# A mixture-of-experts step on one core: buffers in another order, expert homes at multiples of 512 bytes

## What is computed

```python
x = x + gate1 * (mix @ p['w_out'])          # mix: attention | RWKV-7 | HGRN2
h = rms_norm(x, p['norm_ffn_g']) * (1.0 + scale2) + shift2
x = x + gate2 * moe(h)                      # 32 experts, top 4 of them per token
# one expert: gu = xblk @ moe_w_gu[e] + b; act = clamped SwiGLU(gu); act @ moe_w_down[e] + b
```

## The kernel before

| buffer | before | past a multiple of 512 | after | past a multiple of 512 |
|---|---|---|---|---|
| `chosen` (new, 384 bytes) | - | - | 1152 | 128 |
| `ring` (6 homes) | 1152 | 128 | 1536 | 0 |
| `const_sb` | 99456 | 128 | 183808 | 0 |
| home 6 in `const_sb` | 99968 | 128 | 183808 | 0 |
| `param_sb` (2 homes) | 127872 | 384 | 99840 | 0 |
| `proj` (2 homes) | 160640 | 384 | 148992 | 0 |
| `spare` (1 home) | 195456 | 384 | 132608 | 0 |
| `h_nat`, `x_res` | 211840, 220032 | 384 | 212224, 220416 | 256 |

## Time and profile before

### The profile page before, as it was taken

How to read it: one execution, slowest core, us unless ns; L and a number is a source line. 1 busy time by engine, 2 the same in 40 slices (tenths; PEclk the granted TensorE clock), 3 DMA queues, 4 the chain that set the end, 5 groups by cost and what they waited for, 6 DMA issues and landing times.

```text
span 1219.7 us, 17160 instructions
## 1 busy us (share of the span) xinstructions
PE 1151.0 (94%) x7144; PEld 463.6 (38%) x7144; DVE 331.4 (27%) x682; ACT 213.3 (17%) x381; POOL 44.4 (4%) x76
## 2 busy tenths in 40 slices
PE   4999989889999999999999999999999999999996
PEld 0435578755333333333333333333333333333332
DVE  1203777744221111221122111122112211111112
ACT  1212264412111111111111111111111111111112
POOL 0300200000000000000000000000000000000000
PEclk9999999999999999999999999999999999999999
DMA  9999200399999999999999999999999999999994
GB/s 370 324 364 393 79 2 10 147 399 394 406 428 426 426 426 429 426 429 427 427 428 428 427 427 428 428 427 429 426 430 426 429 429 427 426 430 427 427 428 189
DMA packets 44446, 458.91 MB, mean 376 GB/s; under 512 B 5284, under 2 KB 7500, under 8 KB 16624
## 3 DMA queue, kind: packets, MB, share of 16 engines
q1 hardware_dynamic: 41328, 451.46, 88.4%
q0 software_dynamic: 2592, 5.67, 1.6%
q10 hardware_dynamic: 480, 1.13, 0.2%
HBM read 456.76 MB, written 1.47 MB: 376 GB/s over the span
## 4 chain that ended last, share of the span: by engine, by line
PE 74%; DMA 14%; DVE 5%; SPq 4%; issue 2%; ACT 1%; another core or an unknown queue 0%; DVEq 0%; ACTq 0%
PE bank L1308 29%; PE bank L1331 15%; DMA ring<-in_moe_w_gu_dram 12%; PE bank L655 7%; SPq L413 4%; PE bank L1266 4%; PE bank L1250 4%; PE bank L1065 2%; PE bank L1288 2%; DMA ring<-in_w_mod_dram 2%; DVE const_sb L2277 1%; PE bank L630 1%; PE bank L1258 1%; PE bank L643 1%; PE bank L775 1%
## 5 line engine op out<-in xcount | busy, mean ns | idle before, releaser
L1308 PE MATMUL bank<-ring,proj 128*64 128x512 f32 x1024 | 227.8, 594 | 12.7 <-DMA ring<-in_moe_w_gu_dram 12.0
L2268 DVE TENSOR_SCALAR const_sb<-bank 128x512 f32<-128x512 f32 x32 | 22.1, 692 | 426.3 <-PE bank L1308 426.3
L1308 PEld LDWEIGHTS bank<-ring,proj 128*64 128x64 f32 x1024 | 71.8, 137 | 164.8 <-issue 135.1
L1331 PE MATMUL bank<-param_sb,const_sb 128*64 128x512 f32 x512 | 116.9, 598 | 4.8 <-DVE const_sb L2277 4.8
L1331 PE MATMUL bank<-ring,const_sb 128*64 128x512 f32 x512 | 116.9, 598 | 4.8 <-DVE const_sb L2277 4.8
L1694 ACT ACTIVATE const_sb<-const_sb 128x512 f32<-128x512 f32 x32 | 20.2, 630 | 577.0 <-DVE const_sb L2268 577.0
L1308 PE MATMUL bank<-proj 128*64 128x512 f32 x512 | 115.3, 592 | 0.0
L2282 DVE TENSOR_TENSOR x_res<-bank,x_res 128x512 f32<-128x512 f32 x64 | 41.2, 686 | 246.7 <-PE bank L1331 246.7
L655 PE MATMUL bank<-ring,param_sb 128*128 128x512 f32 (+2 forms) x224 | 88.4, 550 | 0.0
L1308 PEld LDWEIGHTS bank<-proj 128*64 128x64 f32 x512 | 36.8, 137 | 73.1 <-issue 73.1
L1266 PE MATMUL bank<-x_res,const_sb 64*128 64x512 f32 x256 | 63.6, 615 | 0.9 <-DVE x_res L2282 0.9
(11 more groups left out here) (357 smaller groups left out, 942.7 us busy)
## 6 DMA issues: line engine op xcount, KB each, us to landing
ring<-in_moe_w_gu_dram SPq DMA_DIRECT2D x64, 2048.0 KB, 39.5
proj<-in_moe_w_gu_dram SPq DMA_DIRECT2D x32, 2048.0 KB, 37.3
ring<-in_moe_w_down_dram SPq DMA_DIRECT2D x32, 2048.0 KB, 36.0
param_sb<-in_moe_w_down_dram SPq DMA_DIRECT2D x32, 2048.0 KB, 37.8
spare<-in_moe_w_gu_dram SPq DMA_DIRECT2D x16, 2048.0 KB, 34.9
const_sb<-in_moe_w_gu_dram SPq DMA_DIRECT2D x16, 2048.0 KB, 36.7
ring<-in_w_mod_dram SPq DMA_DIRECT2D x12, 2048.0 KB, 13.2
ring<-in_w_in_dram SPq DMA_DIRECT2D x5, 2048.0 KB, 11.5
```

The lines of the kernel that those rows point to most:

```text
L1308: mm = pe.matmul(b[CAP * half:CAP * half + CAP, :], xT[:, k % 4, k // 4, :], w[:, 2048 * kc + o + 512 * half:2048 * kc + o + 512 * half + ...
L1331: mm = pe.matmul(b_down[CAP * half:CAP * half + CAP, :], aT[:, k % 4, k // 4, :], w[:, D * kc + 512 * half:D * kc + 512 * half + 512], sta ...
L2268: ts(moe["glu"], b_glu[:, :], LIMIT, None, ALU.min).then_inc(sem("glu_sb"), 1)
```

## The change

Buffers are declared in another order: `ring`, `param_sb`, `spare`, `proj`, and `const_sb` behind them. A new buffer `chosen` of 384 bytes stands ahead of them and takes seven small tables of the expert choice out of `small`, which shrinks from 256 to 160 floats. In `const_sb` the identity matrix `ident` moves from the front to behind the mixers' constants, where it now separates them from `iota`. The table of constants therefore can no longer be loaded by POOL in one DMA, since `ident` is loaded early by ACT: it becomes two, of 4096 and of 416 floats per partition, and those who wait for it wait for both. Nothing else is different: the matmuls, their order, the loads of weights and the homes' numbers are the same.

```diff
 CONST, CONST_W = layout([
-    ("ident", P), ("cent0", P), ("excl0", P), ("cent1", P), ("excl1", P), ("halves0", 2), ("halves1", 2),
+    ("cent0", P), ("excl0", P), ("cent1", P), ("excl1", P), ("halves0", 2), ("halves1", 2),
...
-    ("iota", P), ("ones", P), ("earlier", P), ("iota_e", NE)])
+    ("ident", P), ("iota", P), ("ones", P), ("earlier", P), ("iota_e", NE)])
...
-        ring = sb("ring", [P, NSLOT, SLOT])
         DEAD = CONST["ones"][0] + CAP
         ROUTE = CONST_W + 3 * NE
+        chosen = sb("chosen", [P, 3 * NE])
+        ring = sb("ring", [P, NSLOT, SLOT])
+        low = sb("param_sb", [P, 2 * SLOT])
+        spare = sb("spare", [P, SLOT])
+        rows = sb("proj", [P, 2 * IN_W + 2 * D + KC * NE])
         const = sb("const_sb", [P, ROUTE + 3 * 512 + CAP + 2 * P + 512])
-        low = sb("param_sb", [P, 2 * SLOT])
...
-        rows = sb("proj", [P, 2 * IN_W + 2 * D + KC * NE])
...
-        spare = sb("spare", [P, SLOT])
...
-        small = sb("small", [P, 256])
+        small = sb("small", [P, 160])
...
-            pool.dma_start(const[:, P:CONST_W], a["constants"][:, P:]).then_inc(sem("const_in"), 16)
+            pool.dma_start(const[:, MIXER:MIXER + SLOT], a["constants"][:, MIXER:MIXER + SLOT]).then_inc(sem("const_in"), 16)
+            lo = MIXER + SLOT + P
+            pool.dma_start(const[:, lo:CONST_W], a["constants"][:, lo:CONST_W]).then_inc(sem("const_in"), 16)
...
-            pool.wait_ge(sem("const_in"), 16)
+            pool.wait_ge(sem("const_in"), 32)
...
-                    pe.wait_ge(sem("const_in"), 16)
+                    pe.wait_ge(sem("const_in"), 32)
```

More of the change, by code:

```diff
@@ L70 @@
 CONST, CONST_W = layout([
-    ("ident", P), ("cent0", P), ("excl0", P), ("cent1", P), ("excl1", P), ("halves0", 2), ("halves1", 2),
+    ("cent0", P), ("excl0", P), ("cent1", P), ("excl1", P), ("halves0", 2), ("halves1", 2),
     ("hg0", 6 * P), ("hg1", 6 * P), ("after0", P), ("after1", P), ("eye", DH),
     ("merge", 6 * 3 * DH), ("diag0", DH), ("diag1", DH), ("tri", 4 * DH), ("cos", 32), ("sin", 32), ("rest", 124),
-    ("iota", P), ("ones", P), ("earlier", P), ("iota_e", NE)])
+    ("ident", P), ("iota", P), ("ones", P), ("earlier", P), ("iota_e", NE)])
 MIXER = CONST["cent0"][0]
-assert CONST["iota"][0] - MIXER == SLOT
+assert CONST["ident"][0] - MIXER == SLOT
 PARAM, PARAM_W = layout([
@@ L296, in build @@
         bias_q = moe["bias"][0:97:32]
-        sel_e = carve(small[:, :], [("pos", 2 * NE), ("gate", 2 * NE), ("m8", 16), ("e4", 8), ("a", 16), ("b", 16), ("c", 16),
-                                    ("idxf", 8), ("d", 16), ("cnt", 1), ("cnt_i", 1), ("idx8", 16)])
+        sel_e = carve(small[:, :], [("pos", 2 * NE), ("gate", 2 * NE), ("c", 16), ("cnt", 1), ("cnt_i", 1)])
+        sel_e.update(carve(chosen[:, :], [("m8", 16), ("e4", 8), ("a", 16), ("b", 16), ("idxf", 8), ("d", 16), ("idx8", 16)]))
         tiny = carve(small[:, 0:4 * NE], [("kk", 8), ("kr", 8), ("bonus", 8), ("gn", 8), ("gr", 8), ("hn", 8), ("hr", 8),
@@ L1542, in _ @@
                 act.dma_start(early["c"][KC * k:KC * k + KC, :], src.rearrange("(c p) -> c p", p=P)).then_inc(sem("c_in"), 16)
-            act.dma_start(ident, a["constants"][:, 0:P]).then_inc(sem("ident_in"), 16)
+            act.dma_start(ident, a["constants"][:, MIXER + SLOT:MIXER + SLOT + P]).then_inc(sem("ident_in"), 16)
             act.dma_start(x[:, 0, :], a["x_prompt"][0]).then_inc(sem("x_in"), 16)
```

## The result

| | before | changed |
|---|---|---|
| median of 5 runs | 1223.51 us (1219.15 to 1224.57) | 1212.89 us (1209.72 to 1215.87) |
| ratio, 95% interval | | 0.9919 (0.9899 to 0.9939) |
| span of the profiled execution | 1219.7 us | 1214.2 us |

The kernel became faster by 0.8%. The forecast was 1223.9 us and no change; rival A gave 1216.7 for half of a row's fixed cost and 1208 to 1210 for all of it. The profiled execution is the slowest of the five, so its span shows less of the gain than the median does; under "What was left out" the two parts of the gain are told apart. Two executions far above all others (1705.62 us of the kernel before, 2342.32 us of one variant) are left out of the ratios.

A forecast was written before the change was run, and what follows sets the result against it. PE was taken to bound the early experts and the DMA the last nine. Terms 0 (homes' starts) + 0 (PE, DVE, ACT) + 0.4 us (POOL's added DMA) on 1223.51 gave 1223.9 us, range 1212 to 1230.

The forecast's parts named there:

- rival A: Expert loads: a row's start does cost; half its fixed cost gives 1216.7 us, all 1208 to 1210; chance 0.31.
- Starts of the homes: Expert loads: moving all twelve homes to multiples of 512 bytes changes nothing, 0 us taken.
- the prediction's own mark of 0.013 us: Expert loads: wrong if a load's time differs from 4.90 us by more than this, 2.4 us at the end.
- Both bounds: Expert loads: a row's start costs at most 13.4 to 15.7 us, a cost inside the row at most 16.7.
- PE's own pace: Expert stage: PE leads early with full homes, 27.607 us per expert.
- the DMA as the pace of the end: Last nine experts: homes run empty and loads lead, 29.41 us per expert, 4.90 us per load.
- the conversion of ns per load into time at the end: Stream of 180 expert loads: each nanosecond per load is 0.18 us at the end, up to 16.7 us.
- the ceiling of 16.7 us: Expert stage: all that PE lost to the DMA, 16.7 us; no faster DMA can bring more.
- The 0.4 us for POOL: Before the gate matmuls: the added DMA of constants delays the router weights, +0.4 us out of 0.1 to 0.6.
- rival B: POOL's queue before the router weights: stalls once more, PE 5.2 us later, 1228.7 or 1233 us; chance 0.13.
- Rival C: Expert loads: rows all beginning at the same offset collide with engines' reads, 4.4 us slower, 1228 us; chance 0.10.

The follow-up runs named there:

- half: Changed kernel with a gap of 128 bytes behind the ring, so six homes are at multiples of 512 and six 128 bytes past one; 1219.59 us (one run).

## Why the prediction was wrong

**The step that failed** is the first of the sum, "Starts of the homes": I took 0 out of 0 to 15.7 us. The runs put 4.6 to 5.0 ns per row in its place, x 8 x 180 = 6.6 to 7.2 us; over the whole stream the four unaligned kernels of the table need 889.4 to 890.5 us and the seven aligned ones 881.7 to 883.9, 7.5 us between the means. A load takes 29.20 / 6 = 4.87 us, which passes the prediction's own mark of 0.013 us from 4.90. Both bounds held, and the middle of rival A (5 ns, 7.2 us) was the size.

**Why I missed it.** I compared homes 128 and 384 bytes past a multiple of 512 and found no difference. Both are 128 bytes past a multiple of 256, which is the boundary that counts. The comparison could not have shown the effect. My other argument, that 9 to 11 ns are little for what an engine must do between two rows, was a guess: about half of it was the start. That the measured median, 1212.89 us, still lies inside the outer range of 1212 to 1230 is owed to rival A, not to the forecast.

**What held.** PE's own pace (27.61 us), the DMA as the pace of the end, the conversion of ns per load into time at the end, the ceiling of 16.7 us (not reached: 8.3 us of waits are left), and that PE, DVE and ACT take no notice of the addresses.

**What was left out.** The medians fell by 10.6 and 11.7 us, the stream by 7 to 8. The rest can only lie in the first 300 us, since behind the last expert's fourth piece all whole-row traces need the same 27.3 to 27.9 us. I had counted only the expert stage, but the loads of the front part go into the ring as well: rows of 2,048 bytes pass at 386 to 387 GB/s in the five traces with an unaligned ring and at 411 to 417 in the aligned ones, 84.7 ns per row against 79.5 in the pair of before and changed, 5 to 6 ns. The first expert starts at 303.7 to 313.2 us in the nine traces with an aligned ring and at 306.4 to 314.1 in the five with an unaligned one, with means of 307.4 and 310.3. This difference has the size of the rest, but it is less than either group is wide, so it isn't shown that the rows make it. Most of the spread is there early: one and the same group of matmuls (L633, the one at 130.35 us in the changed kernel) starts at 123.0 to 131.1 us in the fourteen traces, and the first expert 178.8 to 183.1 us behind it.

**The 0.4 us for POOL** and rival B: behind the constants POOL was held back once, not twice, in every trace of two DMAs. The 0.4 us are below what the runs can tell. Rival C, a loss by rows that all begin at one offset, did not occur: all aligned kernels with whole rows show 431 GB/s.

## What to carry to other kernels

Where a stage goes at the DMA's pace, start every destination buffer at a multiple of 256 bytes in its partition; here that was worth 0.8% of the load rate at rows of 16 KB and 6% or more at rows of 2 KB, since the price is per row. Only loads from the chip's memory were tried, with rows whose length is a multiple of 256 bytes. If a trace has no aligned row, list the starts modulo 64, 128, 256 and 512 before comparing buffers: classes that differ by one modulus can be one and the same by another. A fixed cost per row, taken from stretches with rows of different length, is a bound worth a test rather than a floor.

## What the runs showed that I had not expected

- The loss off the boundary is all or nothing at the distances tried: 427.5, 427.6 and 427.5 GB/s at 64, 128 and 192 bytes, 431.0 and 430.9 at 0 and 256.
- Half the homes off the boundary cost about a quarter of the loss in rate (430.2 GB/s between 427.6 and 431.0), not half.
- After pauses of PE of 3.60 us and more the eight gate matmuls took 2.08 us, after one of 3.27 us (half) 1.83, after 2.73 us or less 1.13 to 1.14. From 100 to 104 us the mean granted clock was 0.76 of full speed in the changed kernel (pause 3.60 us) and 1.00 in its second trace (0.65 us): in the front part a longer pause cost its length and a slower restart.
